# Opening with reordered scale, shift and bias products, a first half block split by GpSimd, and TensorE multiplying zeros until x lands

## The reference: what is computed

```
sh1, sc1, g1, sh2, sc2, g2 = split(silu(c) @ mod_w[0] + mod_b[0], 6)    # and the same for c_ctx
h  = rms_norm(x,  norm1_g) * (1 + sc1)  + sh1        # 256 x 1024
hc = rms_norm(cx, norm1_g) * (1 + csc1) + csh1       # 256 x 1024
q, k, v, glu = split(h @ ev_w_in, ...)               # 1024 x 2560
```

## Time and profile before

| | |
|---|---|
| time, median of 3 runs | 1195.97 us (1194.71 to 1196.26) |
| the profiled execution | 1194.39 us, its span 1192.6 us |
| PE busy | 1153.7 us (97%) |
| DVE busy | 692.7 us (58%) |
| ScalarE busy | 486.0 us (41%) |
| GpSimd (POOL) busy | 9.8 us (1%) |
| main DMA queue | 166.23 MB, 41.8% of 16 engines' span |
| chain that ended last | PE 86%, DVE 9%, ACT 3%, issue 1%, DMA 1% |
| mean granted TensorE clock | 0.997 of full speed |

### The profile page before, as it was taken

One profiled execution on the slowest core, in us unless ns is written; L12 is line 12 of the kernel. 1 busy time (PEld: TensorE's weight loads), 2 busy tenths in 40 slices (PEclk: granted clock), 3 DMA queues, 4 the chain that ended last, 5 costly groups with the idle time before them and its releaser, 6 DMA issues.

```text
span 1192.6 us, 17704 instructions
## 1 busy us (share of the span) xinstructions
PE 1153.7 (97%) x7238; PEld 933.8 (78%) x7238; DVE 692.7 (58%) x1160; ACT 486.0 (41%) x744; POOL 9.8 (1%) x18
## 2 busy tenths in 40 slices
PE   5999999999999999999999999999999999999998
PEld 4767776777688888888887767899565798998997
DVE  5489987854443324333323358887789645554455
ACT  4233235643333332222222333367268635443442
POOL 1000000000000000000000000000000000000000
PEclk9999999999999999999999999999999999999999
DMA  9745655025553222333223564244130157655551
GB/s 346 276 142 164 209 204 176 1 66 217 176 177 106 69 72 86 126 109 103 79 80 106 194 217 132 82 140 143 36 127 17 37 179 245 210 178 176 188 171 66
DMA packets 118893, 167.73 MB, mean 141 GB/s; under 512 B 4797, under 2 KB 102695, under 8 KB 114599
## 3 DMA queue, kind: packets, MB, share of 16 engines
q1 hardware_dynamic: 118390, 166.23, 41.8%
q10 hardware_dynamic: 433, 0.51, 0.2%
HBM read 164.37 MB, written 1.05 MB: 139 GB/s over the span
## 4 chain that ended last, share of the span: by engine, by line
PE 86%; DVE 9%; ACT 3%; issue 1%; DMA 1%; SPq 0%; DVEq 0%; ACTq 0%; POOL 0%
PE acc L2138 20%; PE acc L2139 20%; PE acc L2140 20%; PE pmod L2061 2%; PE acc L2222 2%; PE acc L2223 1%; PE acc L2224 1%; PE p L2509 1%; PE p L2507 1%; PE p L2508 1%; PE acc L1998 1%; PE p L1998 1%; DVE Y L1420 1%; DVE sm L1503 1%; DVE w_lo L644 1%
## 5 line engine op out<-in xcount | busy, mean ns | idle before, releaser
L644 DVE TENSOR_TENSOR w_lo<-raw,w_hi 128x1024 fp32r<-128x1024 f32 x222 | 249.0, 1162 | 235.3 <-ACT w_hi L634 235.0
L634 ACT ACTIVATE w_hi<-raw 128x1024 fp32r<-128x1024 f32 (+1 forms) x224 | 212.9, 999 | 408.0 <-PE acc L2140 358.1
L2138 PE MATMUL acc<-Hhi,w_hi 128*128 128x512 f32 (+1 forms) x960 | 326.3, 340 | 4.5 <-DVE w_lo L644 3.9
L2140 PE MATMUL acc<-Hhi,w_lo 128*128 128x512 f32 (+1 forms) x960 | 324.3, 338 | 0.0
L2139 PE MATMUL acc<-Hlo,w_hi 128*128 128x512 f32 (+1 forms) x960 | 324.3, 338 | 0.0
L2138 PEld LDWEIGHTS acc<-Hhi,w_hi 128*128 128x128 f32 x960 | 182.1, 190 | 29.2 <-issue 5.9
L2140 PEld LDWEIGHTS acc<-Hhi,w_lo 128*128 128x128 f32 x960 | 182.1, 190 | 19.6
L2139 PEld LDWEIGHTS acc<-Hlo,w_hi 128*128 128x128 f32 x960 | 182.1, 190 | 19.1
L2138 PE MATMUL acc<-hid_hi,w_hi 128*128 128x512 f32 x248 | 97.9, 395 | 0.1
L2139 PE MATMUL acc<-hid_lo,w_hi 128*128 128x512 f32 x248 | 96.6, 390 | 0.0
L2140 PE MATMUL acc<-hid_hi,w_lo 128*128 128x512 f32 x248 | 96.6, 389 | 0.0
(11 more groups left out here) (387 smaller groups left out, 1593.9 us busy)
## 6 DMA issues: line engine op xcount, KB each, us to landing
raw<-in_mod_w SPq DMA_DIRECT2D x44, 1024.0 KB, 5.2
raw<-in_ffn_w_in SPq DMA_DIRECT2D x44, 1024.0 KB, 5.1
raw<-in_od_w_in SPq DMA_DIRECT2D x15, 1024.0 KB, 5.3
raw<-in_ffn_w_out SPq DMA_DIRECT2D x12, 768.0 KB, 4.5
raw<-in_ev_w_in SPq DMA_DIRECT2D x8, 1024.0 KB, 7.5
raw<-in_od_w_out SPq DMA_DIRECT2D x8, 1024.0 KB, 6.4
raw<-in_ffn_w_out SPq DMA_DIRECT2D x8, 1024.0 KB, 5.0
raw<-in_ev_w_out SPq DMA_DIRECT2D x8, 768.0 KB, 6.0
```

The source lines that it names most:

```text
L634: nc.scalar.activation(w_hi[:, w % 2, c0:c1], raw[:, r % RAW_SLOTS, c0:c1], ACT.Copy)\
L644: nc.vector.tensor_tensor(w_lo[:, w % 2, c0:c1], raw[:, r % RAW_SLOTS, c0:c1], w_hi[:, w % 2, c0:c1].bitcast(F32), ALU.subtract).then_inc( ...
L2138: mm(outs[m], hi[:, j, cols], xh, start=(first and j == 0), stop=False)
L2140: ins = mm(outs[m], lo[:, j, cols], xh, start=False, stop=(last and j == kts - 1))
```

## The change

What it does, engine by engine:
- **Stream order.** The load of unit 8 comes after that of block 2, no longer before it.
- **SP.** The first half of block 0 is loaded ahead of the two `first_mod` tiles of units 0 and 1. Units 2 and 3 get a semaphore each (`scales_loaded1`, `scales_loaded2`); units 0 and 1 still wait for both of their tiles.
- **GpSimd** makes both `w_hi` and `w_lo` of the first half of block 0, after its two squares.
- **ScalarE** no longer makes that `w_hi`, and loads the sigmoid's table with an activation of one column before it waits for the bias.
- **DVE** no longer makes that `w_lo`; copies the sums of units 0 and 1 after the reciprocal; makes the gains for f = 4..7 before, not after, the second halves of w_lo; splits block 2 whole before it takes the bias.
- **PE** multiplies a tile of zeros (`cvec`, 128 x 32 against 256 columns) 14 times before x is waited for. Unit 1 comes after all sums of squares, units 2 and 3 come before block 0, the first two tiles of Hlo are waited for at DVE and not by way of GpSimd, `scales_T(1)` stands in block 0, units 4 to 7 follow block 1 part 0 in one run, `shift_T` stands in block 0 part 1, the shift products come before block 1 part 1, and `bias_columns` stands between its two halves.

```diff
-            if 1 <= n <= 8:
+            if n == 2:
+                stream.append(("mod", 0, 1, 0))
+            if 2 <= n <= 8:
                 stream.append(("mod", 0, 1, n - 1))
...
-   .then_inc(s(f"scales_loaded{i // 2}"), 16)            # in first_scales(i), SP
+   .then_inc(s(f"scales_loaded{max(i - 1, 0)}"), 16)
+            first_block(0, 0, s("first_rows0"))
             first_scales(0)
             first_scales(1)
-            first_block(0, 0, s("first_rows0"))
             first_block(1, 0, s("first_rows1"))
...
+            pool.wait_ge(s("first_rows0"), 16)
+            nc.gpsimd.tensor_copy(w_hi[:, 0, 0:1024], raw[:, 0, 0:1024]).then_inc(hi_split, 1)
+            pool.wait_ge(hi_split, 1)
+            nc.gpsimd.tensor_tensor(w_lo[:, 0, 0:1024], raw[:, 0, 0:1024], w_hi[:, 0, 0:1024].bitcast(F32), ALU.subtract)\
+                .then_inc(lo_split, 1)
...
-            first_hi(0, 0)                                # ScalarE
             first_high(0)
             first_high(1)
+            act.wait_ge(hi_split, 1)
             first_hi(1, 0)
...
                 if n == 0:
+                    step(A(sm[:, 0, 7:8], epsc[:, 0:1], ACT.Sigmoid))
                     act.wait_ge(s("bias_ready"), 1)
...
-            scales_copy(0)                                # DVE
             dve.wait_ge(s("rt_ready"), 1)
             V_.reciprocal(rs0[:, :], rt0[:, :]).then_inc(s("rs_ready"), 1)
+            scales_copy(0)
             first_gains(0)
-            first_lo(0, 0)
             dve.wait_ge(s("rs_spread"), 1)
...
             low0(1)
+            scales_copy(1)
             gained0(3)
+            dve.wait_ge(lo_split, 1)
             first_lo(1, 0)
             low0(3)
+            first_gains(1)
             first_lo(0, 1)
             first_lo(1, 1)
-            scales_copy(1)
-            first_gains(1)
...
                     first_rows()
-                    split(2, parts=(0,))
+                    split(2)
                     first_bias()
                     shifted_low(range(4, KD))
-                    split(2, parts=(1,))
...
+            pe.wait_ge(s("cvec_zero"), 2)                 # PE
+            for _ in range(14):
+                mm(p6[0:32, 0:KD * 32], cvec[:, 0, :], cvec[:, :, :].rearrange("p k c -> p (k c)"), start=True, stop=True)
             pe.wait_ge(s("const_loaded"), 16)
             pe.wait_ge(s("x_loaded"), 32)
...
             for f in range(KD):
                 first_sum(f)
-                if f in (3, 5):
-                    mod_unit(f // 4)
+                if f == 3:
+                    mod_unit(0)
+            mod_unit(1)
             scales_T(0)
             spread_roots(0, T)
+            mod_unit(2)
+            mod_unit(3)
...
                 pe.wait_ge(lo_split, FIRST[0, 0])         # first_two, after
                 for j in range(4):
                     pe.wait_ge(s("h_lo_dve") if j < 2 else s("h_lo"), j + 1)
                     if j == 3:
                         scales_T(1)
                     for m in range(2):
                         column(0, j, m)
                 pe.wait_ge(lo_split, FIRST[1, 0])
                 for j in range(4):
                     for m in range(2):
                         ins = column(1, j, m)
                 ins.then_inc(s("h_used"), 1)
                 for m in range(4, KD):
                     mod_unit(m)
                 pe.wait_ge(lo_split, FIRST[0, 1])
                 for j in range(4, KD):
                     if j == 6:
                         shift_T()
                     pe.wait_ge(s("h_lo"), j + 1)
                     for m in range(2):
                         column(0, j, m)
                 pe.wait_ge(lo_split, FIRST[1, 1])
                 pe.wait_ge(s("shift_ready"), 1)
                 shift_product(0).then_inc(block_done, 1)
                 shift_product(1).then_inc(s("bias_rows"), 1)
                 for j in range(4, KD):
                     column(1, j, 0)
                 bias_columns()
                 for j in range(4, KD):
                     ins = column(1, j, 1)
```

More of the change, by code:

```diff
@@ L478, in first_scales @@
                 sp.dma_start(first_mod[i][:, :].rearrange("p (k n) -> p k n", k=4),
-                             tiles(a["mod_w"][0, rows_:rows_ + 4 * P, cols_:cols_ + 4 * P])).then_inc(s(f"scales_loaded{i // 2}"), 16)
+                             tiles(a["mod_w"][0, rows_:rows_ + 4 * P, cols_:cols_ + 4 * P])).then_inc(s(f"scales_loaded{max(i - 1, 0)}"), 16)
             def first_block(r, part, loaded):
@@ L2018, in mod_unit @@
                 if m < 4:
-                    pe.wait_ge(s(f"scales_loaded{m // 2}"), 32)
+                    pe.wait_ge(s(f"scales_loaded{max(m - 1, 0)}"), 32 if m < 2 else 16)
                     if m == 0:
@@ L2174, in first_two @@
                 for j in range(4):
+                    pe.wait_ge(s("h_lo_dve") if j < 2 else s("h_lo"), j + 1)
+                    if j == 3:
+                        scales_T(1)
+                    for m in range(2):
+                        column(0, j, m)
+                pe.wait_ge(lo_split, FIRST[1, 0])
+                for j in range(4):
+                    for m in range(2):
+                        ins = column(1, j, m)
+                ins.then_inc(s("h_used"), 1)
+                for m in range(4, KD):
+                    mod_unit(m)
+                pe.wait_ge(lo_split, FIRST[0, 1])
+                for j in range(4, KD):
+                    if j == 6:
+                        shift_T()
                     pe.wait_ge(s("h_lo"), j + 1)
@@ L2177, in first_two @@
                         column(0, j, m)
-                mod_unit(2)
-                mod_unit(3)
-                pe.wait_ge(lo_split, FIRST[1, 0])
-                for j in range(4):
-                    if j == 1:
-                        scales_T(1)
-                    for m in range(2):
-                        ins = column(1, j, m)
-                ins.then_inc(s("h_used"), 1)
-                mod_unit(4)
-                mod_unit(5)
-                pe.wait_ge(lo_split, FIRST[0, 1])
-                for j in range(4, KD):
-                    pe.wait_ge(s("h_lo"), j + 1)
-                    for m in range(2):
-                        column(0, j, m)
-                mod_unit(6)
-                mod_unit(7)
                 pe.wait_ge(lo_split, FIRST[1, 1])
-                for j in range(4, KD):
-                    if j == 6:
-                        shift_T()
-                    column(1, j, 0)
                 pe.wait_ge(s("shift_ready"), 1)
@@ L2204, in first_two @@
                 for j in range(4, KD):
-                    if j == 6:
-                        bias_columns()
+                    column(1, j, 0)
+                bias_columns()
+                for j in range(4, KD):
                     ins = column(1, j, 1)
```

## The result

The changed kernel takes 1187.95 us in the median of 4 executions (1187.48 to 1188.69); beside it on the same chip the kernel before took 1195.34 in the median of 4 (1194.09 to 1196.26). The profiled execution took 1187.6 us, its span is 1185.8.

What follows compares the result with a forecast made beforehand. PE, busy 97% of the span, bounds the kernel, with idle time in the opening and block 2. Gains of 0.4 + 0.1 + 0.6 + 2.4 = 3.5 us, 3.6 with GpSimd's hop, give 1192.4 us, range 1189.5 to 1194.6.

Steps and rivals of the forecast that it cites:

- Zeros: PE before x lands: 28 instructions end at 10.7 us, nearly hidden; the first 16 transposes go faster but release nothing.
- Loads: Opening: the second tile for unit 0 lands 1.4 us later, at 17.9; unit 3's tile as before, at 25.5.
- GpSimd's split: Opening: DVE's square of f = 2 waits for GpSimd until 18.6; last sum of squares 1.1 us later.
- first mark: Last sum of squares on PE: from 20.4 to 22.5 us, 2.1 late.
- Clock in the new gap: PE idle until 19.2 us, then partly half clock over sums and units: costs 0.8 to 1.7, taken as 1.0.
- Root to block 0: Last sum to first gained tile 3.3 us for 2.8; that tile at 25.8, block 0 starting at 28.2.
- The second mark: End of block 0 part 0 and units 2 and 3: 34.8 us against 34.9, level.
- Block 1's end: Third mark 60.55 us for 60.95, gaining 0.4, with 0.2 us of stall at unit 7.
- Block 2: PE's waits of 0.61 us for the sigmoid and 2.4 us for w_lo both go.
- The median: Profiled execution 1194.39 becomes 1190.8; it ran 1.6 below the median, so the median 1195.97 becomes 1192.4.
- the clock holds, or DVE gets the port first: Rival for the opening, chance 0.30: full clock gains 4.6 us, without the port's cost too 6.2; 1189.8 to 1191.4.

Runs made afterwards that it cites:

- The kernel with the square held: Changed kernel with DVE's square of f = 2 waiting until GpSimd ended its copy and subtraction: 1188.74 us, ratio 0.9952.
- the one with the extra copy: Changed kernel with one more copy of 1024 columns on GpSimd ahead of the split: 1187.51 us, ratio 0.9940.
- the repeated one: Changed kernel run again unchanged, in the second group, as yardstick: 1187.91 us, ratio 0.9944.

## Why the prediction was wrong

The miss is 4.4 us (1192.4 against 1187.95), and by the traces it has four parts: 2.1 in the opening up to unit 9 (5.7 for 3.6), 0.9 in 316 to 320 us, 0.1 behind that, and 1.2 from the way the median was made. The last: I took the profiled execution's distance to its median, 1.6 us, for a constant; in the changed kernel it is 0.35. So half of the miss is a step of the opening, and the other half is a term that the sum didn't have.

**Zeros.** Right in kind. They ended at 9.27 us (forecast 10.7), 28 in 8.03 us, 16 transposes took 1.94. That they release nothing is shown by the kernel without them.

**Loads.** Right: unit 0 at 17.95 (17.9), the tile of unit 3 for 25.66 (25.5).

**GpSimd's split: the step that failed.** "The square of f = 2 (before at 16.05) waits until 18.6, and the last square ends 2.5 us after that, at 21.05." It ended at 19.41. The copy took 1.03 us and not 1.7, and that square got in between copy and subtraction, which the prediction named as an "if" and did not choose. The port itself behaves as it was read from the earlier trace rows: subtraction 2.34 us alone and 2.69 when issued during a square, square 0.87 when issued during a copy. The rule of the Trainium skill, SBUF — State Buffer, section "Who interferes with whom" (the pair is locked for whole instructions, and issue order decides) agrees with these numbers. The kernel with the square held puts numbers on the two errors: in the assumed order the last square ends at 20.42, so 0.6 of the 1.6 us is the copy's price and 1.0 the order.

This error went through the sum whole: first mark 20.80 for 22.5, first gained tile 24.20 for 25.8, block 0 at 26.67 for 28.2, unit 8 at 58.54 for 60.55. That it belongs there is shown by the two traces with a first gained tile 0.9 us and 0.96 us later, the one with the extra copy and the one without the split: unit 8 is 0.96 and 0.87 later.

What the order costs is another matter. PE stood at unit 0's tile until 17.95 and worked on it until 19.1, so up to there a late square is hidden. The kernel without the split shows this shadow (squares done at 17.86, sums from 19.41 on). The profile of the one with the square held, at full clock, shows 1.0 us of DVE's lateness and no loss at unit 8, but its median is 0.8 higher. So forcing the assumed order brings back at most a small part of the miss: the copy was also cheaper than assumed, and the charge for the clock didn't come on top in that profile.

**Clock in the new gap.** Right in this profile: 3.40 us at 0.50 from 18.6; the repeated one has the same gap and the full clock. The sums of f = 4 to 7 took 1.70 us to unit 1's start, 0.9 in the repeated trace, which is near the 1.0 charged. But a microsecond gained at this mark is worth less: the repeated trace gained 0.7 there, 0.9 at the first gained tile, and kept 0.17.

**Root to block 0.** Right in length: from unit 1's start (20.80) to the first gained tile 3.4 us, forecast 3.3 from the last sum. So that tile came at 24.20 (25.8), block 0 at 26.67 (28.2), at full clock as forecast. The second mark was 32.8 for 34.8: 1.6 from the above, the rest since DVE's chain from the first gained tile to the Hlo of tile 3 took 6.8 us for 7.1, and what followed 1.8 for 1.9.

**Block 1's end.** Unit 8 at 58.54 for 60.55, the same 2.0 us. The stall of 0.2 at unit 7 didn't come here, and was 0.60 in the repeated trace.

**Block 2.** Right: both waits went, and alone in the kernel before this was 3.3 us for 3.0.

**The median.** Here a term was missing, not mis-sized. The 61 executions of the kernel before in the four groups, by their mean clock; their median is 1194.14, while the 1195.97 from which the prediction started is a median of three:

| clock | executions | us | mean |
|---|---|---|---|
| 0.999 | 18 | 1193.22 to 1193.93 | 1193.55 |
| 0.998 | 1 | 1193.89 | 1193.89 |
| 0.997 | 20 | 1193.60 to 1195.04 | 1194.26 |
| 0.996 | 22 | 1195.53 to 1196.31 | 1195.93 |

Filled waits take these away: with block 2's wait filled no execution is over 1194.65, and with three filled all are at 1192.2 to 1192.9. The ten executions of the changed kernel lie at 1187.1 to 1188.7, clocks 0.998 to 1.0. An estimate from these: of the 7.4 us, 1192.53 less 1187.4 (its two executions at 1.0), 5.1, are its schedule, and the other 2.3 are half clock that it meets less often. It compares medians of different groups, and the kernel before differs by 1.5 us between them. For block 0 and block 2 the waits ahead are filled or gone; the norm's waits are not touched. The rival "the clock holds, or DVE gets the port first" had the mechanism in its second half (DVE's square got in first) and 4.6 to 6.2 us, where the traces are 5.7 apart at unit 9; it too lacked this term. What the Trainium skill says in TensorE: Matmul & The Clock Gate, section "HAM oscillation — how this bites in real kernels", that waits between stretches of products throw the clock back, agrees with the filled kernels. It doesn't say in which executions: behind the norm's waits the clock fell in 2 of 15 traces.

**Open.** Which executions fall to half clock behind the same wait, and which don't, no run shows. The upper group of the kernel before is put down to block 2's wait by two things, the trace with zeros alone and the missing group with the filler; no profile of the kernel before itself fell in it. The 0.8 us of the kernel with the square held are not placed either: with half clock in the sums its first gained tile would come later than 24.2 us and be carried on, but no profile shows it. The norm's filler was tried in the kernel before only together with the others.

## What to carry to other kernels

Before a cost is charged to a path, look at what else the waiting engine stands for at that moment: here a tile's landing covered DVE's lateness and made warming up with zeros worthless. Work moved into a wait pays twice, by its own time and by the clock behind the wait; the two units ahead of block 0 were worth 2.1 us with 1.9 us of work. Ask also where slack ends: here the first gained tile gave next to nothing for being earlier than 24.2 us, and cost its full lateness behind that. And where single executions fall into groups, price the waits that can be followed by half clock as a term of its own; a kernel's profile shows one member of the group only.

## What was not expected of the hardware

- GpSimd copied 128 x 1024 elements to fp32r in 1.03 us, the time that ScalarE takes for them (1.05), while its subtraction of the same size takes 2.34.
- More work on TensorE can shorten a kernel: 8 products of zeros before block 0 took 1.8 us off the median, 17 in three waits took 1.3 us off it in their group and narrowed the executions from 2.6 to 0.64 us; no change lies outside both intervals.
- The same wait can be followed by either clock: that of 2.4 us by the full one in the earlier trace rows and by 0.50 in another execution, those of 1.27 and 0.62 us in the second norm by half clock in 2 of 15 traces.
